# Expert results, two tiles of weights and the first two products: whole rows or halves of the tokens

## What is computed

```python
# end of the first block
    y = lax.ragged_dot(jax.nn.silu(a) * b, w2, sizes)
    y = (y * weights[order][:, None]).astype(h.dtype)
    return jax.ops.segment_sum(y, tok, num_segments=N)
...
        x = x + gt2 * y
# beginning of the second block
        h = rms_norm(x, g_mix_pre[l])
        z = h @ w_in[l]
        u_pool = z[..., :c0]
```

## Time and profile before

| | |
|---|---|
| median of three executions | 3487.85 us (3486.68 to 3489.31) |
| the profiled execution | 3490.16 us, its span 3488.3 us |
| granted TensorE clock, mean | 0.960 |
| TensorE busy | 3179.9 us, 91% |
| VectorE busy | 2186.2 us, 63% |
| ScalarE busy | 1312.6 us, 38% |
| GpSimd busy | 1000.7 us, 29% |

### The profile page before, as it was taken

How to read it: one execution, slowest core, us unless ns; L and a number is a source line. 1 busy time by engine, 2 the same in 40 slices (tenths; PEclk the granted TensorE clock), 3 DMA queues, 4 the chain that set the end, 5 groups by cost and what they waited for, 6 DMA issues and landing times. The chain is left out here.

```text
span 3488.3 us, 44976 instructions
## 1 busy us (share of the span) xinstructions
PE 3179.9 (91%) x15137; PEld 2526.0 (72%) x15137; DVE 2186.2 (63%) x2689; ACT 1312.6 (38%) x1717; POOL 1000.7 (29%) x501
## 2 busy tenths in 40 slices
PE   5889989788889499999959999699899999999998
PEld 4658867565677488888848788578668888888877
DVE  6588885677543899999965655743365235235366
ACT  3245423566412388888831265100131000000142
POOL 2323332000142011111114333245324444444432
PEclk9999999899999799999979999799999999999999
DMA  6313221231151699999961122032221111111312
GB/s 225 76 44 91 79 54 49 73 121 37 49 165 63 256 380 380 378 379 385 365 253 51 61 76 82 28 100 91 84 90 48 49 48 48 48 48 48 105 40 67
DMA packets 351491, 446.15 MB, mean 128 GB/s; under 512 B 32990, under 2 KB 235660, under 8 KB 351380
## 3 DMA queue, kind: packets, MB, share of 16 engines
q1 hardware_dynamic: 336676, 410.08, 34.5%
q10 hardware_dynamic: 5344, 17.83, 1.6%
q0 software_dynamic: 9360, 16.80, 1.3%
HBM read 397.40 MB, written 58.75 MB: 131 GB/s over the span
## 5 line engine op out<-in xcount | busy, mean ns | idle before, releaser
L410 PE MATMUL acc<-Ah,whi 128*128 128x512 f32 x2336 | 935.8, 401 | 80.0 <-DVE Al L604 21.4
L411 PE MATMUL acc<-Al,whi 128*128 128x512 f32 x2336 | 918.2, 393 | 0.0
L412 PE MATMUL acc<-Ah,wlo 128*128 128x512 f32 x2336 | 917.9, 393 | 0.0
L382 POOL TENSOR_TENSOR whi<-wraw,one 128x1024 fp32r<-128x1024 f32 (+2 forms) x208 | 390.0, 1875 | 1833.9 <-PE acc L412 1514.5
L410 PEld LDWEIGHTS acc<-Ah,whi 128*128 128x128 f32 x2336 | 443.7, 190 | 204.9 <-issue 71.1
L384 POOL TENSOR_TENSOR wlo<-wraw,whi 128x1024 fp32r<-128x1024 f32 (+2 forms) x208 | 530.1, 2548 | 16.3
L411 PEld LDWEIGHTS acc<-Al,whi 128*128 128x128 f32 x2336 | 444.2, 190 | 96.3 <-issue 5.6
L412 PEld LDWEIGHTS acc<-Ah,wlo 128*128 128x128 f32 x2336 | 443.2, 190 | 95.0
L1861 DVE TENSOR_TENSOR mlo<-mraw,mhi 128x1024 fp32r<-128x1024 f32 x256 | 307.0, 1223 | 38.0 <-ACT mhi L1810 22.8
L1810 ACT ACTIVATE mhi<-mraw 128x1024 fp32r<-128x1024 f32 x256 | 268.1, 1062 | 78.9 <-PE acc L1755 53.6
L410 PE MATMUL acc<-Bh,whi 128*128 128x512 f32 x640 | 251.3, 393 | 8.9 <-POOL wlo L384 8.9
(11 more groups left out here) (497 smaller groups left out, 4760.3 us busy)
## 6 DMA issues: line engine op xcount, KB each, us to landing
mraw<-in_exp_w SPq DMA_DIRECT2D x512, 256.0 KB
mraw<-in_exp_w SPq DMA_DIRECT2D x128, 512.0 KB, 11.6
wraw<-in_w_in SPq DMA_DIRECT2D x72, 512.0 KB, 3.7
wraw<-in_w_up SPq DMA_DIRECT2D x48, 512.0 KB, 3.8
TT<-in_ada_w SPq DMA_DIRECT2D x32, 512.0 KB, 3.8
TT<-gates SPq DMA_DIRECT2D x32, 512.0 KB, 4.5
wraw<-in_w_down SPq DMA_DIRECT2D x24, 512.0 KB, 3.9
adaraw<-in_ada_w SPq DMA_DIRECT2D x16, 512.0 KB
```

Source lines behind the costliest of these rows:

```text
L382: ch(pool.tensor_tensor(whi[:, r, 0:k, 0:m], wraw[:, r, 0:k, 0:m], one[:, 0:1].unsqueeze(2).broadcast_to([P, k, m]), ALU.mult))
L410: pe.matmul(o, whi[:, r, j, 0:m], ih[:, k0 + j, cols], start=(j == 0), stop=False)
L411: pe.matmul(o, whi[:, r, j, 0:m], il[:, k0 + j, cols], start=False, stop=False)
L412: last = pe.matmul(o, wlo[:, r, j, 0:m], ih[:, k0 + j, cols], start=False, stop=(j == k - 1))
```

## The change

It has four parts, all at the seam.

1. SyncE loads the first two weight tiles of the second block behind `RG`, in the loop's end. ScalarE makes `whi` of them behind the last `YO`, VectorE `wlo`. GpSimd no longer does it.
2. The first scaling of each block of `G12` is an activation on ScalarE (`scale_rows`), with a count `y_scaled` for VectorE, which keeps the addition. In the second stage ScalarE's scalings stand between its `Ah` instructions, and VectorE's additions between its `C` and `Al`.
3. Turning, `C`, `Ah` and `Al` go by halves of 512 tokens: all eight feature tiles of tokens 0 to 511, then of 512 to 1023. A turn is four transposes into one of four PSUM half tiles. TensorE begins when four blocks are summed.
4. The first two products go by halves: first product first half, second product first half, first product second half, second product second half. The turns of the second half's first four tiles stand behind steps 2 to 5 of the second product's first half. `w_used` is counted at the two products' second halves, so it keeps its order.

GpSimd's `memset` of `bdr` now waits for all 16 turns. The diff also has three functions (`mean_half`, `root_half`, `newton_half`) that nothing calls; they are left out here.

```diff
+    def product_half(pe, r, h, ih, il, done, ready=None, after=None, hi=whi, lo=wlo):
+        for j in range(KD):
+            if ready is not None:
+                pe.wait_ge(ready[0], ready[1] + j + 1)
+            o = acc[r][:, tokens(h)]
+            pe.matmul(o, hi[:, r, j, :], ih[:, j, tokens(h)], start=(j == 0), stop=False)
+            pe.matmul(o, hi[:, r, j, :], il[:, j, tokens(h)], start=False, stop=False)
+            last = pe.matmul(o, lo[:, r, j, :], ih[:, j, tokens(h)], start=False, stop=(j == KD - 1))
+            if after is not None and j < KD - 1:
+                after(j)
+        last.then_inc(done, 1)
...
         sp.dma_start(RG[:], tiles(x1T)).then_inc(S("x1T_in"), 16)
+        for j in range(2):
+            load(sp, N0["pool"] + j, j, W2[:, :, j * P:(j + 1) * P])
...
         result(end)
+        for j in range(2):
+            act.wait_ge(w_land[j], landed[N0["pool"] + j])
+            act.activation(whi[:, j, :, :], wraw[:, j, :, :], ACT.Copy).then_inc(S("first_hi"), 1)
...
         place(end)
+        for j in range(2):
+            dve.wait_ge(S("first_hi"), j + 1)
+            dve.tensor_tensor(wlo[:, j, :, :], wraw[:, j, :, :], whi[:, j, :, :].bitcast(F32), ALU.subtract)\
+               .then_inc(w_lo, 1)
...
     def sum_rows(dve, b):
         ch = chain(dve, "dve")
-        dve.wait_ge(S(f"y_in{b}"), 16)
-        ch(dve.tensor_scalar(G12[:, 0, b, :], G12[:, 0, b, :], WTOK[:, 0, b:b + 1], None, ALU.mult))
+        dve.wait_ge(S("y_scaled"), b + 1)
...
+    def scale_rows(act, b):
+        act.wait_ge(S(f"y_in{b}"), 16)
+        act.activation(G12[:, 0, b, :], G12[:, 0, b, :], ACT.Copy, scale=WTOK[:, 0, b:b + 1]).then_inc(S("y_scaled"), 1)
...
-        for j in range(4):
+        pool.wait_ge(S("y_turned"), 2 * KD)
+        ch(pool.memset(bdr[:], 0.0))
+        pool.sem_inc(S("bd_zero"), 1)
+        for j in range(2, 4):
             split(pool, N0["pool"] + j, j % 2, landed[N0["pool"] + j])
...
+        pe.wait_ge(S("y_sum"), NB // 2)
+        for m in range(4):
+            turn(0, m)
...
+        product_half(pe, 0, 0, Ah, Al, S("pool_half"), (S("n3_lo"), 0), turns_ahead(0))
+        product_half(pe, 1, 0, Ah, Al, S("pool_half"), None, next_turns)
+        product_half(pe, 0, 1, Ah, Al, w_used, (S("n3_lo"), KD), turns_ahead(1))
+        product_half(pe, 1, 1, Ah, Al, w_used)
         pe.wait_ge(S("n3_sum"), KD)
...
+        scale_rows(act, 3)
+        for h in range(2):
+            for m in range(KD):
+                act.wait_ge(S("x2_done"), KD * h + m + 1)
+                high_half(act, "n3", m, h, gain3)
+                if h == 0 and m in (0, 2, 4, 5):
+                    scale_rows(act, 4 + (m + 1) // 2)
...
+        for h in range(2):
+            for m in range(KD + 1):
+                if m < KD:
+                    i = KD * h + m
+                    dve.wait_ge(S("y_turned"), i + 1)
+                    ch(dve.scalar_tensor_tensor(C[:, m, tokens(h)], turn_banks[i % 4][:], MOD[:, 40 + m:41 + m],
+                                                RG[:, m, tokens(h)], ALU.mult, ALU.add))
+                    dve.sem_inc(S("x2_done"), 1)
+                if m:
+                    low_half(dve, "n3", m - 1, h, gain3)
+                if h == 0 and m in (1, 3, 5, 6):
+                    sum_rows(dve, 4 + m // 2)
```

More of the change, by code:

```diff
@@ L596, in newton_step, with tokens, mean_half, root_half @@
         ch(dve.scalar_tensor_tensor(r if to is None else to, t, 1.5, r, ALU.add, ALU.mult))
+    def tokens(h):
+        return slice(h * HALF, (h + 1) * HALF)
+    def product_half(pe, r, h, ih, il, done, ready=None, after=None, hi=whi, lo=wlo):
[9 more added lines that the diff above has]
+        last.then_inc(done, 1)
+        if after is not None:
+            after(KD - 1)
+    def mean_half(pe, h, squares, first, last, done):
+        pe.matmul(Y[:, tokens(h)], meanD[:], squares[:, tokens(h)], start=first, stop=last).then_inc(done, 1)
+    def root_half(act, tag, r, h, mean, done="_mean"):
+        ch = chain(act, "act")
+        act.wait_ge(S(tag + done), mean)
+        ch(act.activation(r[:, tokens(h)], Y[:, tokens(h)], ACT.Ln, bias=eps[:]))
+        ch(act.activation(r[:, tokens(h)], r[:, tokens(h)], ACT.Exp, scale=-0.5))
+        act.sem_inc(S(tag + "_root"), 1)
+    def newton_half(dve, ch, tag, r, t, h):
+        r, t, y = r[:, tokens(h)], t[:, tokens(h)], Y[:, tokens(h)]
+        dve.wait_ge(S(tag + "_root"), h + 1)
+        ch(dve.scalar_tensor_tensor(t, r, -0.5, r, ALU.mult, ALU.mult))
+        ch(dve.scalar_tensor_tensor(t, y, EPS, t, ALU.add, ALU.mult))
+        ch(dve.scalar_tensor_tensor(r, t, 1.5, r, ALU.add, ALU.mult))
+    def high_half(act, tag, m, h, gain):
+        act.activation(Ah[:, m, tokens(h)], C[:, m, tokens(h)], ACT.Copy, scale=gain(m)).then_inc(S(tag + "_hi"), 1)
+    def low_half(dve, tag, m, h, gain):
+        dve.wait_ge(S(tag + "_hi"), KD * h + m + 1)
+        dve.scalar_tensor_tensor(Al[:, m, tokens(h)], C[:, m, tokens(h)], gain(m), Ah[:, m, tokens(h)].bitcast(F32),
+                                 ALU.mult, ALU.subtract).then_inc(S(tag + "_lo"), 1)
     def split_rows(tag, m, act=None, dve=None, gain=None):
@@ L1923, in _ @@
             sp.dma_start(G12[:, :, b, :], ys.rearrange("(k b p) n -> b p k n", k=2, p=P)[b]).then_inc(S(f"y_in{b}"), 16)
+    def scale_rows(act, b):
+        act.wait_ge(S(f"y_in{b}"), 16)
+        act.activation(G12[:, 0, b, :], G12[:, 0, b, :], ACT.Copy, scale=WTOK[:, 0, b:b + 1]).then_inc(S("y_scaled"), 1)
+    @block.scalar
+    def _(act):
+        for b in range(3):
+            scale_rows(act, b)
     @block.vector
@@ L1989, in _, with turn, turns_ahead, after @@
     def _(pe):
[L1990 to L1994, removed]
-            last.then_inc(S("y_turned"), 1)
[L1997 to L2005, removed]
+        def turn(h, m):
+            i = KD * h + m
+            if i >= 4:
+                pe.wait_ge(S("x2_done"), i - 3)
+            for b in range(4):
+                last = pe.transpose(turn_banks[i % 4][:, b * P:(b + 1) * P],
+                                    G12[:, 0, 4 * h + b, m * P:(m + 1) * P], ident[:])
+            last.then_inc(S("y_turned"), 1)
+        def turns_ahead(h):
+            def after(j):
+                if j + 4 < KD:
+                    turn(h, j + 4)
+            return after
+        def next_turns(j):
+            if 2 <= j < 6:
+                if j == 2:
+                    pe.wait_ge(S("y_sum"), NB)
+                turn(1, j - 2)
+        pe.wait_ge(S("y_sum"), NB // 2)
+        for m in range(4):
+            turn(0, m)
+        for r in range(2):
+            pe.wait_ge(w_lo, N0["pool"] + r + 1)
+            pe.wait_ge(acc_free[r], take(r))
+        product_half(pe, 0, 0, Ah, Al, S("pool_half"), (S("n3_lo"), 0), turns_ahead(0))
+        product_half(pe, 1, 0, Ah, Al, S("pool_half"), None, next_turns)
+        product_half(pe, 0, 1, Ah, Al, w_used, (S("n3_lo"), KD), turns_ahead(1))
+        product_half(pe, 1, 1, Ah, Al, w_used)
         pe.wait_ge(S("n3_sum"), KD)
@@ L2028, in _ @@
         ch = chain(dve, "dve")
-        for b in range(3, NB):
-            sum_rows(dve, b)
+        sum_rows(dve, 3)
         dve.wait_ge(S("x1T_in"), 16)
[L2032 to L2039, removed]
+        for h in range(2):
+            for m in range(KD + 1):
+                if m < KD:
+                    i = KD * h + m
+                    dve.wait_ge(S("y_turned"), i + 1)
[6 more added lines that the diff above has]
+                    sum_rows(dve, 4 + m // 2)
         for m in range(KD):
```

9 lines of the change are left out of this document (3 added, 6 removed).

## The result

| | before | after |
|---|---|---|
| median of six executions | 3488.58 us (3485.12 to 3489.78) | 3501.94 us (3500.38 to 3504.75) |
| ratio | 1 | 1.0040, 95% interval 1.0030 to 1.0051 |
| the profiled execution | 3490.16 us, span 3488.3 us | 3501.02 us, span 3499.2 us |
| granted clock, mean | 0.960 | 0.958 |

What follows compares the result with a forecast made beforehand. The prediction followed VectorE's chain to the end of its adds of squares, which holds up TensorE's mean and all behind it. +5.2 (wait), +3.6 (adds) and +2.85 (clock) made +11.7 on 3487.85: 3499.5 us, range 3491 to 3504.

Steps and rivals of the forecast that it cites:

- Loop's end: End of the expert loop: the added weight copies, subtractions and loads fit into idle time and cost 0.
- To the first `C`: Second stage's start: first `C` at 1797.4 instead of 1805.07, a head start of 7.7 us.
- First half: VectorE's sums and eight half pairs of `C` and `Al` at 1.6 us each, ending at 1815.6.
- The wait: VectorE idles 6.2 us (3.6 to 7.0) for a turn behind 15 products; `Al` ends at 1834.8, +5.2.
- The adds: VectorE's seven adds of squares: the fourth product's weight split now lands among them, lengthening two more, +3.6 us.
- The clock: TensorE, idle 11 us before the mean, falls to half clock and loses 2.85 us behind it.
- The sum: Whole kernel: +5.2, +3.6 and +2.85 make +11.7 us, for 3499.5.
- keep its clock: Rival: TensorE at full clock through the first half's gaps and before the mean; +6.2, 3494; 0.24 with its relatives.
- overlap as drawn: Rival: first half done while rows land, no wait for the turn; -6, 3481.8; 0.07 with anything below +2.
- Half clock throughout: Rival: TensorE at half clock through the second half too; +15, 3503; 0.09 together with a late scatter.
- a late landing of the weights or a held-up scatter: Rival at the loop's end: adds 1 to 3 us to any case; late scatter shares 0.09 with half clock.
- the mark: End of VectorE's seven adds of squares, before the mean; forecast at 1852.3 for 1843.49, +8.8.

Runs made afterwards that it cites:

- e2: Changed kernel with the second half's first four turns behind steps 5 and 6 of the first product's first half, the next four behind the second product's; 3493.73 us, 1.0018.
- e1: Changed kernel, but GpSimd splits the fourth product's weights only when the last sum of squares is added; 3499.53 us, 1.0031 of the kernel before.
- e8: Changed kernel plus 46 matmuls, whose results nobody reads, in TensorE's wait ahead of the mean; 3498.00 us, 1.0030 of the kernel before.
- e3: Changed kernel with the third and fourth products ahead of the mean and ScalarE emptying accumulators between its squares; 3487.61 us, 1.0000 of the kernel before.
- e9: Changed kernel with early second-half turns, third and fourth products before the mean, and both products' first halves stepped together; 3483.36 us, 0.9985 of the kernel before.
- e5: Kernel before with only the first scaling of every block moved to ScalarE, whole tiles; 3489.56 us, 1.0006 of the kernel before.
- e6: Kernel before with only the first two weight tiles loaded and split in the loop's end, GpSimd relieved of them; 3485.96 us, 0.9999.
- e7: Kernel before, nothing halved, with the first weights split in the loop's end and the third and fourth products ahead of the mean; 3485.93 us, 0.9993.
- e4: Changed kernel with the second half's turns early and the third and fourth products ahead of the mean; 3485.37 us, 0.9989 of the kernel before.

## Why the prediction was right

Point by point, the prediction's figure first.

- **Loop's end, 0.** In the profiles this holds. From the last `YO` to the issue of the loads of `ys` the kernel before takes 5.21 us and the changed one 5.22. So neither ScalarE's copies nor the loads delayed the last scatter. Before, then after:

```profile
1772.61 1.02 ACT L1821 ACTIVATE YO<-acc 128x1024 f32<-128x1024 f32 x1 [6.61 <-PE acc L1774]
1777.82 6.89 SPq L1923 DMA_DIRECT2D G<-ys  x8
...
1772.97 1.02 ACT L1866 ACTIVATE YO<-acc 128x1024 f32<-128x1024 f32 x1 [6.62 <-PE acc L1819]
1778.19 7.04 SPq L1974 DMA_DIRECT2D G<-ys  x8
```

- **To the first `C`, 7.7 us of head start.** 7.75, counted from the issue of the loads. The table load stands at 1792.58 for 1.28 us, ahead of the fourth scaling, as reckoned; the first `C` came at 1797.69 for 1797.4.
- **First half, end at 1815.6.** It ended at 1816.2. An instruction of 512 columns took 0.75 us where one of 1024 took 1.28, so halving saves 0.53 us and not 0.64, near the 0.54 reckoned. Half pairs start 1.56 us apart for 1.6.
- **The wait, 6.2 us (3.6 to 7.0).** 5.72 and 0.39 us. Ninth `C` at 1821.93 for 1821.9; last `Al` at 1834.87 for 1834.8, or, counted from the issue of the loads, 4.88 us later than before for 5.2. That it is the turn's place in TensorE's order is shown by e2, where it shrank to 1.24 us and gave back 5.0 us. That the times meet to a tenth is in part luck. The seventh `Al` was ready 0.5 us later than reckoned, and the 15 products took 0.4 us less, the last four at full clock. And the half clock was there, but the reason given for it does not hold for all steps: with three products a step TensorE was at half from 1803.5 to 1806, at 1.00 from 1808 to 1812, and at half again only from the step of the seventh `Al` on. At 0.23 us each the 15 products would have taken 3.4 us, where they took 5.7; so about 2.3 us of the wait are the clock's, an estimate that no run tests by itself.
- **The adds, +3.6.** Measured +3.5, and e1 took back 3.4 of it by moving the one split. The split came at 1842.27, not at 1841 as reckoned: the second product was done by 1841.3, but GpSimd was at the third product's split until 1842.3, which the reckoning had left out. It met two adds all the same. By the rule of the Trainium skill (page "SBUF — State Buffer", section "SBUF: two separate sides") with full durations the term would have been 4.3. The trace agrees with the rule: GpSimd's first instruction ends at 1839.00, the add that stood behind it from 1837.39 ends at 1840.09, a plain 1.1 us later, and GpSimd's next from 1839.08 ends at 1842.32, 2.2 us behind that add, near its 2.35 alone. So the two engines take turns, and what an add loses is not the whole of the other's instruction but what is left of it: 1.46 and 1.92 us here.
- **The clock, +2.85.** e8 gives 2.59. The third product's first matmul starts 2.79 us behind the mean's start, where e8 has 1.42: 1.4 us are lost at the mean and the rest in the first matmuls behind it. Full pace came back at 1858.0, 5.6 us after work began, for 5.7 in the earlier trace rows.
- **The sum, +11.7.** The stretch grew by 11.03. Taken away one at a time, the three terms gave back 5.0 (e2, at the last `Al`), 3.4 (e1, in the adds) and 2.6 (e8, in the stretch), 11.0 in all. The medians differ by 13.4, with 10.5 to 17.8 in the interval; whether the 2.4 between stretch and medians is more than scatter is open. In the two profiled executions the times differ by 10.86.

The rivals fell by rows of the changed kernel. TensorE did not keep its clock: 0.50 from 1816 to 1820 and from 1852 to 1856. The halves did not overlap as drawn, since half a pair costs 1.56 and not under 1.27 us, and there was a wait. Half clock throughout did not come: in the chain the last four of the 15 products are 0.23 us apart. Nor did a late landing of the weights or a held-up scatter add to it (5.22 us for 5.21, above).

One sentence of the prediction was too narrow: that whatever moves the mark moves all that follows. It holds for this order of TensorE's work alone. e3 leaves the mark late and takes the whole loss away by putting two products ahead of it. Nor do halves by themselves make a kernel slower: e9 keeps them and is faster than the kernel before.

What stays open: the place of the loop's end, which moved by up to 4.6 us between profiles, also of kernels that are alike up to it (a part of that is traced in the last section); and e5's and e6's single gains of 1.2 and 1.4 us, which stand in the stretches of one profile each and not in the timed ratios.

## What to carry to other kernels

When work is cut in halves so that two engines overlap, look at what stands ahead of the second half's first instruction in the in-order queue of the engine that feeds it: here 15 matmuls in front of one turn cost 5.0 us (e2) of a head start of 7.75. Then follow the earlier finish to the engines that it sets free, since a split that starts sooner can land on the very chain that sets the end; and put work that does not need the late result ahead of the wait for it. With the late mark of the changed kernel that was worth more than all else (11.9 us, e3), in the kernel before only 1.3 (e7 against e6).

## What the runs showed of the hardware

The granted clock did not follow the length of a single wait. TensorE's timeline of the changed kernel, at the last two steps of the first half, and the windows around them:

```profile
1812.57 0.50 PE L607 MATMUL acc<-Ah,whi 128*128 128x512 f32 x1 [2.02 <-DVE Al L638]
1815.56 0.80 PE L607 MATMUL acc<-Ah,whi 128*128 128x512 f32 x1 [2.03 <-DVE Al L638]
...
1812.00:1816.00 4.00, 1.40 (x4) 0.92 (x5) 3.71 (x5) 1.16 (x2) 0.00 (x0) 0.69 0.00 0
1816.00:1820.00 4.00, 4.00 (x11) 3.03 (x10) 0.21 (x1) 0.00 (x0) 0.00 (x0) 0.50 0.02 4
```

After a wait of 2.02 us the matmul ran at the full 2.4 GHz (0.50 us in the record), after the next, of 2.03 us, at 1.2 GHz (0.80 us). Between the two TensorE had three matmuls. So it was in e1, e3 and e8 too, which have the same order there: 0.50 or 0.51 us behind the first of these waits, 0.79 behind the second. In e9, with six matmuls a step in the same place, the clock stayed at 1.00. More work in the same steps kept the clock up; at which point it is lost was not measured.

Nor did the same instructions with the same wait always end alike. The last product of the expert loop stands behind a wait of 2.92 us in all eleven profiles. Its first two matmuls in the kernel before, then in e1:

```profile
1766.86 0.49 PE L1772 MATMUL acc<-mhi,HTh 128*128 128x512 f32 x1 [2.92 <-DVE HTl L1900]
1767.19 0.40 PE L1773 MATMUL acc<-mlo,HTh 128*128 128x512 f32 x1
...
1766.70 0.79 PE L1817 MATMUL acc<-mhi,HTh 128*128 128x512 f32 x1 [2.92 <-DVE HTl L1948]
1767.29 0.63 PE L1818 MATMUL acc<-mlo,HTh 128*128 128x512 f32 x1
```

In seven profiles the clock stayed up and the last `YO` came 5.75 to 5.78 us behind the first of these matmuls. In e1 the clock was at half from the start and it came after 8.49 us; in e3, e4 and e9 the clock fell within the product, and it came after 7.40 or 7.41. So 1.6 to 2.7 us of a single execution hang on this: a part of the 4.6 us by which the loop's end moved, and a reason to count from a mark behind it. All four kernels that lost the clock there have the weight loads of the change in the loop's end, but so have five of the seven that kept it. Whether the loads make the loss more frequent, which would be a small cost of the change outside the stretch, one profile of each kernel does not show.
